# A fused mLSTM, cross-attention and SwiGLU block: the gate columns ride behind the first value strip, the first strip and the late input tiles come in another order, and every large tile starts at a multiple of 512 bytes

## The chip, the cores and the metric

The kernel runs on one core of a Trainium2 chip. The metric is the device time of one execution in microseconds, as the median of several runs. The engines are called by their names in the profile: PE (TensorE, the matrix products), PEld (its weight loads), DVE (VectorE), ACT (ScalarE), POOL (GpSimd) and SP (SyncE, which issues all DMAs here).

## What is computed

One transformer block on x (1024 tokens by 1024 features) with a memory of 256 tokens, all in float32:

```python
h = x
h = h + mlstm_mix(rmsnorm(h, norm_mix), a_w_in, a_conv_w, a_gate_b, a_norm, a_w_out)
h = h + cross_attn(rmsnorm(h, norm_x), rmsnorm(mem, norm_mem), x_w_q, x_w_kv, x_w_o)
h = h + swiglu(rmsnorm(h, norm_ffn), f_w_gate, f_w_up, f_w_down)
out = rmsnorm(h, norm_final)

def mlstm_mix(xn, w_in, conv_w, gate_b, norm_g, w_out):      # 4 heads, key width 128, value width 256
    qk, v, o, g = split(xn @ w_in, [1024, 2048, 3072])       # g: 8 columns, an i and an f gate per head
    qk = silu(causal_dwconv(qk, conv_w))                     # 4 taps
    g = g + gate_b
    i_pre, log_f = g[:4], log_sigmoid(g[4:])
    # a scan over the tokens in chunks, with stabilised exponential gates made of i_pre and cumsum(log_f)
    return (head_rmsnorm(scan(q, k, v, i_pre, log_f), norm_g) * sigmoid(o)) @ w_out
```

## The kernel before

**Products in three terms.** Every large matrix product is made of three float32r products: each operand a is split into a high part ah (a copy written as float32r) and a low part al = a - ah, and a*b is taken as ah*bh + al*bh + ah*bl. ACT writes the high parts, DVE or POOL the low ones. `XH` and `XL` hold the normalised input, transposed (8 blocks `k` of 128 features by 1024 tokens), `WH` and `WL` two weight strips each, used in turn.

**Strips.** The projections are done in strips of 256 weight columns, in the order of the list `STRIPS`: it begins with qk 0, v 0, o 0, then qk 1, v 1, o 1, wo 0, and so on. For each strip SP loads 1 MB into `raw`, ACT copies it into `WH` (`split_hi`, L878), and DVE makes `WL` in two halves (L1606) while PE works on the strip before. A strip has groups `r`, each of which fills one of the PSUM banks 0 to 3 (`NB` = 4) with 24 matmuls of 512 columns, or, for v, with 48 of 256 columns: there the tokens are stationary and the weights are moving. v and o are taken out of PSUM by ACT, qk by DVE, with the convolution (`evac`, L1541 to L1554).

**Order.** It is written out by hand: each engine runs the same loop over `STRIPS` and groups, and at fixed places does the side work that `PARTS` names (`run_parts`): the gates, the scan of the head before, the norms. The scan of head 0 begins with group 0 of the strip qk 1, on PE, ACT and DVE.

**The start.** SP issues four tiles of x (128 tokens each, `xin`), the small vectors, strip 0, the gate weights `wg_raw` (8 columns) and their bias, and then tiles 4 to 7 into the same four buffers, each after PE has turned and ACT has squared the tile that was in it. PE transposes a tile (`turn_x`, L2146), DVE (L1571) and ACT (L1074) take it out of PSUM into `xT`. ACT sums the squares (L883), POOL makes 1/rms (L804), PE spreads it over the partitions (`spread`, L2083), and then `pieces(c, k)` makes one block: DVE multiplies xT, gain and 1/rms (L1463), ACT writes `XH` (L972), and `XL` is made by DVE for even `k` (L1445) and by POOL for odd `k` (L811); c = 0 is the first half of the tokens, c = 1 the second. PE consumes the blocks as they come, in `two_groups` (L1961 to L1963), which does strip qk 0, first half, then second half, with the transposes of the tiles 6 and 7 between.

**The gates.** A product of its own, in `gates` step 0, at the first group of v 0: `wgp` holds the 8 high gate columns, the 8 low ones and zeros, as a stationary operand of 128 columns, against `XH` and `XL` as moving operands (L1974, L1975, 32 matmuls). DVE copies the 16 result rows (L1288), PE transposes them (L1980). Steps 1 to 5 are a chain of short operations that goes back and forth between PE, DVE and ACT; they stand at v 0 groups 2 and 3 and o 0 groups 0, 1 and 3:

```python
for step, (kind, r) in enumerate([("v", 0), ("v", 2), ("v", 3), ("o", 0), ("o", 1), ("o", 3)]):
    part(kind, 0, r, ("gates", step, None))
```

**Places.** All tiles are laid out by hand in one array of SBUF. It starts at byte 1152 of a partition, so that `xT`, `XH`, `XL`, `raw`, `WH`, `WL`, `QK`, `SG`, `YH`, `YL` and `VV` start 128 bytes past a multiple of 512; the part for late tiles (`late_at`, with `W2A`, `VMH` and `KMH`) starts 384 bytes past one.

## Time and profile before

| | |
|---|---|
| median of 3 runs | 1408.13 us (1406.9 to 1408.98) |
| the profiled execution's own time | 1408.76 us |
| its span, first to last instruction | 1407.0 us |
| PE busy | 1373.6 us, 98% of the span |
| PEld / DVE / ACT / POOL busy | 83% / 68% / 35% / 15% |
| TensorE clock granted, mean | 0.992 of full speed |
| DMA | 156.44 MB, mean 111 GB/s |

A busy PE here means that a matmul was in its pipe; since matmuls overlap, how fast it works is read from how many start in a stretch. The profiled execution spent 1.76 us outside the span.

### The profile page before, as it was taken

The numbers are of one execution on the slowest core, as the hardware profiler recorded it, in microseconds if no ns is written. First come the engines' busy times: TensorE is split into PE (matmuls) and PEld (weight loads), VectorE is DVE, ScalarE is ACT, GpSimd is POOL, SyncE is SP. The second block draws the span as 40 slices with busy tenths as digits, with TensorE's granted clock in tenths as the row PEclk, the third lists the DMA queues.
The fourth block names the chain that finished last, engine by engine and source line by source line (L and its number), as shares of the span: only waits on it lengthen the run. The fifth ranks groups of instructions, "written<-read, shape, count | busy, mean of one in ns | idle before, by whom it ended". The sixth has DMA issues, their size and how long they took to land.

```text
span 1407.0 us, 18269 instructions
## 1 busy us (share of the span) xinstructions
PE 1373.6 (98%) x6897; PEld 1165.9 (83%) x6897; DVE 954.8 (68%) x1678; ACT 493.4 (35%) x870; POOL 209.2 (15%) x228
## 2 busy tenths in 40 slices
PE   7999999999999999999999999999999998999997
PEld 6988888889888888888877888888888886888887
DVE  5838458458477884554677976677787778877765
ACT  6323213213335453222344533343444433222222
POOL 4101201201313000000004000000000004444441
PEclk9999999999999999999999999999999999999999
DMA  5110111201313211010132132244444449799702
GB/s 181 34 57 31 56 36 31 60 30 31 106 61 101 80 60 61 31 61 23 38 120 105 47 114 96 74 165 164 142 140 160 153 165 374 246 311 318 236 31 120
DMA packets 109256, 156.44 MB, mean 111 GB/s; under 512 B 6449, under 2 KB 67953, under 8 KB 109169
## 3 DMA queue, kind: packets, MB, share of 16 engines
q1 hardware_dynamic: 109168, 155.28, 32.9%
q8 instruction: 55, 0.90, 0.3%
q14 instruction: 33, 0.26, 0.1%
HBM read 112.79 MB, written 42.47 MB: 110 GB/s over the span
## 4 chain that ended last, share of the span: by engine, by line
PE 88%; DVE 6%; issue 2%; DMA 1%; SPq 1%; ACT 1%; POOL 0%; POOLq 0%; DVEq 0%; ACTq 0%
PE PS L1898 14%; PE PS L1899 14%; PE PS L1900 14%; PE PS L2220 8%; PE PS L2218 8%; PE PS L2219 8%; PE PS L2248 4%; PE PS L2250 4%; PE PS L2249 4%; PE PS L2040 1%; PE PS L2044 1%; PE PS L2042 1%; DVE SG L1430 1%; PE PS L1961 1%; DVE xT L1528 1%
## 5 line engine op out<-in xcount | busy, mean ns | idle before, releaser
L1898 PE MATMUL PS<-XH,WH 128*128 128x512 f32 (+1 forms) x448 | 175.4, 391 | 3.3 <-issue 3.3
L1899 PE MATMUL PS<-XL,WH 128*128 128x512 f32 (+1 forms) x448 | 169.7, 379 | 0.0
L1900 PE MATMUL PS<-XH,WL 128*128 128x512 f32 (+1 forms) x448 | 169.4, 378 | 0.0
L1528 DVE TENSOR_TENSOR xT<-PS,xT 128x512 f32<-128x512 f32 x128 | 87.5, 688 | 47.0 <-PE PS L1900 46.6
L1740 DVE TENSOR_TENSOR xT<-PS,xT 128x512 f32<-128x512 f32 x120 | 80.9, 688 | 43.8 <-PE PS L2250 43.0
L1898 PE MATMUL PS<-YH,WH 128*128 128x512 f32 x256 | 101.5, 396 | 0.7 <-issue 0.7
L1898 PEld LDWEIGHTS PS<-XH,WH 128*128 128x128 f32 x448 | 85.5, 191 | 19.3 <-issue 4.4
L1900 PE MATMUL PS<-YH,WL 128*128 128x512 f32 x256 | 99.8, 390 | 0.0
L1899 PE MATMUL PS<-YL,WH 128*128 128x512 f32 x256 | 99.7, 390 | 0.0
L1900 PEld LDWEIGHTS PS<-XH,WL 128*128 128x128 f32 x448 | 85.4, 191 | 16.0
L1899 PEld LDWEIGHTS PS<-XL,WH 128*128 128x128 f32 x448 | 85.5, 191 | 14.6
L1898 PE MATMUL PS<-WH,XH 128*128 128x256 f32 x320 | 92.6, 289 | 2.0 <-issue 2.0
L1900 PE MATMUL PS<-WH,XL 128*128 128x256 f32 x320 | 90.5, 283 | 0.0
L1899 PE MATMUL PS<-WL,XH 128*128 128x256 f32 x320 | 90.5, 283 | 0.0
L845 POOL TENSOR_TENSOR W2A<-raw,W2A 128x512 fp32r<-128x512 f32 x20 | 27.5, 1377 | 386.6 <-ACT W2A L1185 386.6
L1680 DVE TENSOR_TENSOR U<-PS,U 128x512 f32<-128x512 f32 x50 | 33.6, 688 | 55.7 <-PE PS L2220 55.7
L1606 DVE TENSOR_TENSOR WL<-raw,WH 128x1024 fp32r<-128x1024 f32 x54 | 65.8, 1226 | 3.8 <-ACT WH L878 3.8
L1898 PEld LDWEIGHTS PS<-WH,XH 128*128 128x128 f32 x320 | 61.2, 191 | 2.9 <-issue 2.4
L2220 PE MATMUL PS<-XH,WA 128*128 128x512 f32 x160 | 62.2, 389 | 0.0
L2218 PE MATMUL PS<-XH,WA 128*128 128x512 f32 x160 | 62.2, 389 | 0.0
L2218 PE MATMUL PS<-XH,WB 128*128 128x512 f32 x160 | 62.2, 389 | 0.0
L2220 PE MATMUL PS<-XH,WB 128*128 128x512 f32 x160 | 62.2, 389 | 0.0
(396 smaller groups left out, 3522.7 us busy)
## 6 DMA issues: line engine op xcount, KB each, us to landing
forms_hi<-HS SPq DMA_DIRECT2D x56, 256.0 KB, 2.4
raw<-in_f_w_up_dram SPq DMA_DIRECT2D x11, 1024.0 KB, 5.8
rawE<-in_f_w_gate_dram SPq DMA_DIRECT2D x10, 1024.0 KB, 6.0
raw<-in_f_w_down_dram SPq DMA_DIRECT2D x40, 256.0 KB, 3.8
raw<-in_a_w_in_dram SPq DMA_DIRECT2D x8, 1024.0 KB, 5.3
forms_lo<-U SPq DMA_DIRECT2D x32, 256.0 KB, 2.5
XH<-forms_hi SPq DMA_DIRECT2D x16, 512.0 KB, 6.5
XL<-forms_lo SPq DMA_DIRECT2D x12, 512.0 KB, 7.0
```

Of the source, the lines that this page charges most:

```text
L1528: v.tensor_tensor(xt, PS[:, g % NB, :], xt, ALU.add).then_inc(s_fd, 1)
L1606: last = v.tensor_tensor(WL[:, (n + 1) % 2, at], raw_of(n + 1)[:, at], WH[:, (n + 1) % 2, at].bitcast(F32), ALU.subtract)
L1740: v.tensor_tensor(x, bank_of(g, which), x, ALU.add).then_inc(s_ee, 1)
L1898: mm(dst, wh, xh, start=(k == 0), stop=False)
L1899: mm(dst, wh, xl, start=False, stop=False)
L1900: last = mm(dst, wl, xh, start=False, stop=(k == len(tiles) - 1))
L2218: mm(bank, w[:, i, 0, at], xh[:, kk, :], start=start, stop=False, skip_group_check=True)
L2219: mm(bank, w[:, i, 0, at], xl[:, kk, :], start=False, stop=False, skip_group_check=True)
L2220: last = mm(bank, w[:, i, 1, at], xh[:, kk, :], start=False, stop=stop, skip_group_check=True)
L2248: mm(bank, w[:, i, 0, at], xh[:, u, :], start=start, stop=False, skip_group_check=True)
L2249: mm(bank, w[:, i, 0, at], xl[:, u, :], start=False, stop=False, skip_group_check=True)
L2250: last = mm(bank, w[:, i, 1, at], xh[:, u, :], start=False, stop=stop, skip_group_check=True)
```

## The change

- **Gates in the first value strip.** The strip v 0 is now the first one and qk 0 the second. Its high weights lie in a tile of their own, `GW`, in rows of 272 columns: 256 value columns, 8 high gate columns, 8 low ones. For each block k and tile of 128 tokens, `first_value` does three matmuls: XH by 272 columns, XL by 264, XH by the 256 columns of `WL`. Each of the 8 token tiles has a bank of its own (the eighth takes the fourth's after that is taken out), and comes out of PSUM in two copies, 256 columns to `VV` and 16 to `zg`. The product `wgp`, its copy `grow` and its transposes are gone; the gate chain has 5 steps, at qk 0 group 2 and at o 0 groups 0 to 3.
- **Another start.** Tiles 4 to 7 of x get their own places (`xlate`, where `YH` and `YL` are later), and are issued as soon as tiles 0 to 3 have landed; strip v 0 is loaded in two halves, the second behind tile 5. ACT splits it in two halves, POOL makes the low part of the first half and DVE that of the second. Tiles 4 to 7 are taken out of PSUM by ACT alone, in two halves each, through three banks in turn, and are turned one by one between the blocks k = 0 to 3 of `first_value(0)`. All sixteen `XL` blocks are made by DVE.
- **Places.** `LINE` is 512 in place of 128, and the array's large tiles start at byte 1536, so that `xT` to `VV`, `acc`, `ident` and `late_at` all start at a multiple of 512; the small ones lie ahead of them. `ones`, `tri` and `cmax` lie behind `zg`, behind the gate columns; a column of ones (`one`) takes the place of `ones[:, 0:1]` in `sumsq`.

```diff
-LINE = 128
+LINE = 512
-    STRIPS = [("qk", 0), ("v", 0), ("o", 0)]
+    STRIPS = [("v", 0), ("qk", 0), ("o", 0)]
+    GATED = AT["v", 0]
+    ngroups = lambda n: TT if n == GATED else NGROUPS[STRIPS[n][0]]
+    bank_at = lambda n, r: (0, 1, 2, 3, 4, 5, 6, 3)[r] if n == GATED else GI[n, r] % NB
-    for step, (kind, r) in enumerate([("v", 0), ("v", 2), ("v", 3), ("o", 0), ("o", 1), ("o", 3)]):
-        part(kind, 0, r, ("gates", step, None))
+    part("qk", 0, 2, ("gates", 0, None))
+    for step in range(1, 5):
+        part("o", 0, step - 1, ("gates", step, None))
-        who = "dve" if c in (2, 3) or (c < 2 and k % 2 == 0) or (c == 5 and k >= KT // 2) else "pool"
+        who = "dve" if c in (2, 3) or c < 2 or (c == 5 and k >= KT // 2) else "pool"
+        small_at = (nc.sbuf_base + 31) // 32 * 32
+        base = (small_at + 4 * SMALL + LINE - 1) // LINE * LINE
...
+        GW = sb_at("GW", [P, KT, SW + 2 * GCOLS], late_at, F32R)
+        zg = sb_at("zg", [P, TT, 2 * GCOLS], late_at + 8704)
+        ones = sb_at("ones", [P, P], late_at + 11264)
...
SP:
-            for t in range(TT):
-                if t >= 4:
-                    sp.wait_ge(s_turn, t - 3)
-                    sp.wait_ge(s_sq, t - 3)
-                sp.dma_start(xin[t % 4], x_t[t]).then_inc(s_xin[t % 4], 16)
...
+            sp.dma_start(dst[:, 0:KT // 2], src[:, 0:KT // 2]).then_inc(s_w0, 16)
+            sp.dma_start(wg_raw, cols(a_w_in, G0, 2 * H)).then_inc(s_wg, 16)
+            for t in range(4):
+                sp.wait_ge(s_xin[t], 16)
+                sp.dma_start(xlate[t], x_t[4 + t]).then_inc(s_xin[t], 16)
+                if t == 1:
+                    sp.dma_start(dst[:, KT // 2:], src[:, KT // 2:]).then_inc(s_wdma, 16)
+            sp.dma_start(gbias[:, :], a_gate_b[0:1, :].to_broadcast([P, 2 * H])).then_inc(s_gb, 16)
+            sp.wait_ge(s_wl0, 1)
ACT:
+            split_first(0)
             for k in range(KT):
                 pieces(0, (k,))
+                if k == 0:
+                    split_first(1)
+                if 1 <= k <= 4:
+                    late_tile(k + 3)
+                if 2 <= k <= 5:
+                    square_x(k + 2)
+            for k in range(KT):
+                pieces(1, (k,))
+                if 1 <= k <= 4:
+                    evac(GATED, FIRST_OUT[k - 1])
+                if 4 <= k <= 5:
+                    split_second(k - 4)
DVE:
+            pieces(0, (0,))
+            pieces(0, (1,))
+            dve.wait_ge(s_wg, 16)
+            link(v.tensor_copy(GW[:, :, SW:SW + GCOLS], wg_raw))
+            v.tensor_tensor(GW[:, :, SW + GCOLS:], wg_raw, GW[:, :, SW:SW + GCOLS].bitcast(F32), ALU.subtract).then_inc(s_wgs, 1)
+            pieces(0, (2, 3))
+            dve.wait_ge(s_whi, 1)
+            v.tensor_tensor(by_k(WL[:, 0, second]), by_k(raw[:, second]), GW[:, KT // 2:, 0:SW].bitcast(F32),
+                            ALU.subtract).then_inc(s_wlo, 1)
+            pieces(0, range(4, KT))
             pieces(1, range(KT))
PE:
+            def first_value(half, between=None):
+                wide, narrow = SW + 2 * GCOLS, SW + GCOLS
+                for kk in range(KT):
+                    if between is not None:
+                        between(kk)
+                    lo_ready(pe, half, kk)
+                    for r in range(half * NT, half * NT + NT):
...
+                        mm(bank[:, 0:wide], xh, GW[:, kk, 0:wide], start=(kk == 0), stop=False, skip_group_check=True)
+                        mm(bank[:, 0:narrow], xl, GW[:, kk, 0:narrow], start=False, stop=False, skip_group_check=True)
+                        last = mm(bank[:, 0:SW], xh, col(GATED, kk, 0, SW)[1], start=False, stop=(kk == KT - 1),
+                                  skip_group_check=True)
-                if step == 0:
-                    pe.wait_ge(s_wgs, 1)
-                    for half in range(NHALF):
-                        for kk in range(KT):
...
-                            mm(PS[:, NB + half, :], wgp[:, kk, :], xh, start=(kk == 0), stop=False)
-                            last = mm(PS[:, NB + half, :], wgp[:, kk, :], xl, start=False, stop=(kk == KT - 1))
             def late_tiles(kk):
+                if 1 <= kk <= 3:
+                    turn_x(4 + kk)
                 if kk == 4:
                     wait_strip(0)
                 if kk == 7:
                     spread(0, 1)
+            turn_x(4)
             pe.wait_ge(s_wl0, 1)
+            pe.wait_ge(s_wgs, 1)
+            first_value(0, late_tiles)
+            first_value(1)
```

## Rows read from the trace of the kernel before

**Rows 1.** The page, busy time of PE.

```profile
PE 1373.6 (98%) x6897; PEld 1165.9 (83%) x6897; DVE 954.8 (68%) x1678; ACT 493.4 (35%) x870; POOL 209.2 (15%) x228
```

**Rows 2.** Table by stretch: PE, PEld, DVE, ACT, POOL busy (starts), clock, DMA share, GB/s.

```profile
17.80:44.50 26.70, 25.77 (x119) 20.83 (x118) 20.31 (x33) 15.77 (x25) 14.01 (x12) 0.96 0.15 45
44.50:51.80 7.30, 7.30 (x34) 6.02 (x33) 7.12 (x10) 0.96 (x2) 0.00 (x0) 1.00 0.03 6
...
76.10:98.90 22.80, 22.80 (x101) 18.27 (x100) 9.75 (x38) 5.73 (x9) 0.00 (x0) 1.00 0.15 47
98.90:1407.00 1308.10, 1283.91 (x6393) 1087.85 (x6391) 895.45 (x1558) 454.05 (x811) 187.95 (x198) 0.99 0.33 112
52.00:62.00 10.00, 10.00 (x86) 10.00 (x85) 9.47 (x19) 3.55 (x4) 0.00 (x0) 1.00 0.31 102
```

**Rows 3.** The same table, two stretches at half the clock.

```profile
16.55:19.97 3.42, 3.42 (x13) 3.03 (x13) 3.38 (x5) 2.76 (x7) 3.14 (x3) 0.50 0.47 192
753.80:760.70 6.90, 6.90 (x20) 5.55 (x20) 0.16 (x1) 0.00 (x0) 1.20 (x2) 0.51 0.40 139
```

**Rows 4.** The timeline of the start: start us, length us, engine, line, operation.

```profile
5.67 3.23 SPq L592 DMA_DIRECT2D QK<-in_a_w_in_dram  x1
...
10.94 1.78 SPq L585 DMA_DIRECT2D VQ<-in_x_dram  x4
...
12.71 1.91 ACT L878 ACTIVATE WH<-raw 128x2048 fp32r<-128x2048 f32 x1 [2.64 <-DMA raw<-in_a_w_in_dram]
...
14.70 2.96 POOL L766 TENSOR_TENSOR WL<-raw,WH 128x512 fp32r<-128x512 f32 x2 [3.23 <-ACT WH L878]
...
15.13 1.09 PE L2146 MATMUL PS<-ident,VQ 128*128 128x128 f32 x8 [2.96 <-DMA VQ<-in_x_dram]
15.18 1.35 DVE L1445 TENSOR_TENSOR XL<-SG,XH 128x512 fp32r<-128x512 f32 x1 [1.29 <-ACT XH L972]
15.57 1.04 ACT L883 ACTIVATE QK<-VQ 128x1024 f32<-128x1024 f32 x1
...
16.61 0.57 ACT L1074 ACTIVATE xT<-PS 128x512 f32<-128x512 f32 x1
...
17.90 0.77 PE L1961 MATMUL PS<-XH,WH 128*128 128x512 f32 x1
```

**Rows 5.** The timeline, one block of the second half.

```profile
32.09 1.29 ACT L972 ACTIVATE XH<-SG 128x512 fp32r<-128x512 f32 x2 [3.03 <-DVE SG L1463]
...
32.75 0.69 DVE L1445 TENSOR_TENSOR XL<-SG,XH 128x512 fp32r<-128x512 f32 x1
33.36 1.40 DVE L1463 SCALAR_TENSOR_TENSOR acc<-xT,vcols,PS 128x512 f32<-128x512 f32 x2
```

**Rows 6.** The timeline of DVE, convolutions of group 0 and group 3.

```profile
41.06 0.75 DVE L1541 TENSOR_SCALAR acc<-PS,vcols 128x512 f32<-128x512 f32 x1
...
44.20 0.16 DVE L1554 COPY small<-PS 128x3 f32<-128x3 f32 x1
...
55.11 0.75 DVE L1541 TENSOR_SCALAR acc<-PS,vcols 128x512 f32<-128x512 f32 x1
...
59.02 0.16 DVE L1554 COPY small<-PS 128x3 f32<-128x3 f32 x1
```

**Rows 7.** The timeline of DVE, gate steps 1 and 4.

```profile
64.08 0.23 DVE L1295 COPY ks<-PS 128x64 f32<-128x64 f32 x1 [1.37 <-PE PS L1980]
...
67.14 1.22 DVE L1606 TENSOR_TENSOR WL<-raw,WH 128x1024 fp32r<-128x1024 f32 x1
...
82.12 0.19 DVE L1324 COPY hs<-PS 128x32 f32<-128x32 f32 x1 [3.04 <-PE PS L1992]
...
86.28 0.27 DVE L1336 TENSOR_SCALAR hs<-SG,hs 32x128 f32<-32x128 f32 x1
```

**Rows 8.** The groups by line and shape: busy us, mean ns of one.

```profile
L2040 PE MATMUL PS<-VV,wT 128*128 128x257 f32 x64 | 19.2, 382 | 0.0
L2042 PE MATMUL PS<-Cst,qs 128*128 128x257 f32 x56 | 16.7, 380 | 0.0
```

More of the change, by code:

```diff
@@ L54, in build_block @@
     FIRST, FREED, took = {}, [], {"act": 0, "dve": 0, "up": 0}
-    GROUPS = [(n, r) for n, (kind, _) in enumerate(STRIPS) for r in range(NGROUPS[kind])]
+    GATED = AT["v", 0]
+    assert GATED == 0
+    ngroups = lambda n: TT if n == GATED else NGROUPS[STRIPS[n][0]]
+    GROUPS = [(n, r) for n in range(len(STRIPS)) for r in range(ngroups(n))]
     at = GROUPS.index((NF, 0))
@@ L219, in build_block @@
         half_neg = few(NT)
+        one = few(1)
         nsum, nmean, nrms = few(NHALF, NT), few(NHALF, NT), few(NHALF, NT)
@@ L282, in build_block @@
         sqsum = [None, halves(QK[:, 1, 1, :]), SG[:, :, HALF:]]
-        wgp = YH[:, 0, :].rearrange("p (k g) -> p k g", k=KT)
-        grow = VV[0:4 * H, 1].rearrange("p t d -> p (t d)")[:, 0:S]
+        XT4 = sb_at("XT4", [P, 4, S], place["YH"])
+        xlate = [XT4[:, t, :] for t in range(4)]
         fout = xin
@@ L827, in _ @@
                 kind, h = STRIPS[n]
-                for r in range(NGROUPS[kind]):
+                for r in range(ngroups(n)):
                     run_parts(n, r, todo)
@@ L885, in gates @@
             def gates(step, b):
-                if step == 1:
+                if step == 0:
                     act.wait_ge(s_gd, 1)
@@ L1076, in _, with split_first @@
-            square_x(0)
-            square_x(1)
-            square_x(2)
-            square_x(3)
-            split_hi(0)
+                for unit in range(2):
+                    dst, src = tile_of(t, unit)
+                    sc.activation(dst, src, ACT.Copy).then_inc(s_xta, 1)
+            def split_first(u):
+                k = slice(u * KT // 2, (u + 1) * KT // 2)
+                src = raw[:, u * KT * P:(u + 1) * KT * P].rearrange("p (k n) -> p k n", k=KT // 2)
+                if u == 0:
+                    act.wait_ge(s_w0, 16)
+                    sc.activation(GW[:, k, 0:SW], src, ACT.Copy).then_inc(s_w0h, 1)
+                else:
+                    act.wait_ge(s_wdma, 16)
+                    sc.activation(GW[:, k, 0:SW], src, ACT.Copy).then_inc(s_whi, 1)
@@ new lines, in split_second @@
+            def split_second(u):
+                if u == 0:
+                    act.wait_ge(s_wdma, 16 * DMAS[1][1])
+                at = slice(u * KT * P, (u + 1) * KT * P)
+                last = sc.activation(WH[:, 1, at], raw[:, at], ACT.Copy)
+                if u:
+                    last.then_inc(s_whi, 1)
+            for k in range(KT):
[4 more added lines that the diff above has]
+                    split_second(k - 4)
@@ L1090, in _ @@
                 kind, h = STRIPS[n]
-                for r in range(NGROUPS[kind]):
+                for r in range(ngroups(n)):
                     if r == 0 and held and STRIPS[held[0][0]][0] == "q":
@@ L1595, in _ @@
                 which = 1 if kind == "wo" else 2
-                for r in range(NGROUPS[kind]):
+                for r in range(ngroups(n)):
                     run_parts(n, r, todo)
@@ L1609, in _ @@
                             last.then_inc(s_wlo, 1)
+                        elif n == GATED:
+                            last.then_inc(s_wl0, 1)
                     if kind == "mv":
@@ L1889, in wait_bank, with product @@
                 if g >= NB:
-                    who, count = FREED[g - NB]
+                    who, count = FREED[NT - 1 if TT <= g < TT + NT - 1 else g - NB]
                     pe.wait_ge({"act": s_fa, "dve": s_fd, "up": s_hf}[who], count)
-            def product(dst, tiles, before=None):
+            def product(dst, tiles, before=None, second=None):
                 for k, ((wh, wl), (xh, xl)) in enumerate(tiles):
+                    if second is not None and k == len(tiles) // 2:
+                        wait_strip(second)
                     if before is not None:
@@ L1945, in group @@
                     order = range(KT) if before is None else EARLY + LATE
-                    last = product(bank, [(col(n, kk, r % 2), xpart(kk, at, HALF)) for kk in order], before)
+                    last = product(bank, [(col(n, kk, r % 2), xpart(kk, at, HALF)) for kk in order], before,
+                                   second=1 if (n, r) == (1, 0) else None)
                 last.then_inc(s_mm, 1)
@@ L2067, in sumsq @@
                 for t in range(NT):
-                    last = mm(X2[:, t:t + 1], sqsum[which][:, half, t * P:(t + 1) * P], ones[:, 0:1], start=True, stop=True)
+                    last = mm(X2[:, t:t + 1], sqsum[which][:, half, t * P:(t + 1) * P], one, start=True, stop=True)
                 last.then_inc(s_ssq, 1)
@@ L2176, in _ @@
                     run_parts(n, r, todo)
-                    if r == 0:
+                    if r == 0 and n == 1:
+                        pe.wait_ge(s_whi, 2)
+                        pe.wait_ge(s_wl0, 2)
+                    elif r == 0:
                         wait_strip(n)
```

218 lines of the change are left out of this document (101 added, 117 removed).

## The prediction

> **What bounds the kernel now.** I read the page first: PE is busy for 98% of the span [rows 1]. A busy PE need not be fast, so the second view is the table by stretch, for how many matmuls start. From 44.5 to 51.8 us the 32 matmuls of 512 columns of the gate product fill the stretch with next to nothing left, 0.227 us from start to start; from 52 to 62 us some 84 of 256 columns fill it, 0.12 us each [rows 2]. Hence a column costs (0.227 - 0.12) / 256 = 0.42 ns, and each matmul about 0.013 us on top. From 44.5 to 51.8 and from 76.1 to 98.9 us PE has no idle time at all, and over the remaining 1308.1 us it is idle for 24 [rows 2]. So until 98.9 us, where strip qk 1 and with it the scan of head 0 begin, a column that PE need not stream is time won, unless another engine is late with what PE wants next. Third, the timeline of the start: PE waits for tile 4 of x until 15.13 us and begins its first product at 17.90 us, when POOL has the first half of WL (14.70 + 2.96) [rows 4]. From there to 44.5 us it is idle for 0.93 of 26.7 us [rows 2].
>
> The code behind the start of qk 1 is the same before and after but for places, so I work out when qk 1 starts: 98.9 us before.
>
> **The gates' columns.** Removed: 32 matmuls of 512 columns, the stretch 44.5 to 51.8 us, 7.3 us [rows 2], and 8 transposes of 16 columns: between nothing and 8 x 0.12 = 1 us, the start-to-start time of the 256-column matmuls; they are far narrower, so I take 0.5. Added: in each of 64 steps (8 blocks, 8 token tiles) 16 + 8 = 24 more columns, 64 x 24 x 0.42 ns = 0.65 us. By this alone the change gains about 7.1 us. DVE's copy of `grow` goes, ACT gets eight small copies; neither is on PE's path there.
>
> **The start.** SP issues x0 to x3, the vectors and now only half of the strip, so the gate columns, whose issue alone takes 3.23 us [rows 4], go out some 0.5 us earlier, at 5.1 us, and tile 4 behind them at about 8.4 instead of 10.94 us. Before, tile 4 landed at 15.13 us, 4.2 us after its issue into empty queues [rows 4]; that would make it 12.6 now, but it also waits behind half a strip and the gate columns: I take 13.2 us. Each further 0.5 MB I estimate at 1.25 us: tile 5 at 14.4, the second half of the strip at 15.7, tiles 6 and 7 at 17 and 18. The first half strip lands at about 10.8 us (the whole one was there at 12.71). ACT splits it in half of 1.91 us, to 11.8 us, and POOL needs 2.96 us for its two subtractions [rows 4]: 14.8 us. DVE's four tile copies are as before; I estimate their end at 12.3 us. Then come two blocks' products at 0.7 us [rows 5], one XL block, and the gate columns. That XL block took 1.35 us at 15.18 us while POOL worked, and takes 0.69 us at 32.75 us without it [rows 4, 5]. I take the long value, since POOL's second subtraction overlaps it again: `s_wgs` at 15.7 us. **First product at 15.7 us, before 17.9.**
>
> The Trainium skill (SBUF — State Buffer, Who interferes with whom) says that a DVE instruction with two SBUF inputs and a GpSimd instruction that reads SBUF block each other for the whole instruction. The row of 1.35 us agrees. By that rule moving all sixteen XL blocks to DVE also rids them of POOL, which has no work left after 15 us.
>
> **First half of the tokens.** PE needs per block 4 x (0.12 x 3 + 24 x 0.42 ns) = 1.48 us, eight times 11.8 us, and 3 late tiles of 1.0 us and the spread of 0.6 us: 15.5 us. But ACT now takes out both halves of each late tile. From the landing of the second half strip at 15.7 us it has, in its own order: that split, 0.95 us; seven XH blocks at 0.6 us; eight half tiles at 0.57 us; four squares at 1.04 us [rows 4, 5]: 13.9 us, so XH of block 7 is there at 29.6 us. Followed in order, block 4 is ready on ACT at 24.5, block 5 at 27.3, block 6 at 28.95 us; each needs 0.7 us more on DVE. PE has done block 3 at 24.8 us, waits 0.4 us for block 4, 1.3 us for block 5 and 0.1 for block 6, ends block 6 at 31.1 us, spreads, and ends block 7 at 33.2 us. DVE is no bound here: 1.4 us a block.
>
> **Second half.** Block 0 comes after the spread: 0.7 us DVE, 0.64 us ACT, 0.7 us DVE [rows 5], so PE starts it at 33.9 us (before there was a like wait). Then DVE makes a block in 1.4 us [rows 5] where PE needs 1.48, and DVE's share of 0.7 us more per odd block, taken over from POOL, is hidden; ACT has the blocks, four outputs and the next split, 10 us in all. 33.9 + 11.9 = 45.8 us: **strip qk 0 starts at 45.8 us**. WL of qk 0, DVE's last work before, is ready by halves at about 45 and 46 us, and PE wants the second half only after four blocks.
>
> **Strips qk 0 and o 0.** Let T be the start of qk 0. Four groups of 24 matmuls with 0.1 us for the change of group: 22.1 us. DVE is the one that is late now. The groups end at T + 5.7, 11.2, 16.6 and 22.1 us. A convolution took 3.3 us in groups 0 and 1 (41.06 to 44.36) and 4.1 us in 2 and 3 (55.11 to 59.18) [rows 6]. At group 2 DVE first does the old gate step 1, 3.1 us with its trip to ACT (64.08 to 67.14), and half of a WL, 1.15 us [rows 7]; so convolution 2 ends at T + 23.5, `finish_qk` of group 1 at 24.1, convolution 3 at 28.2, `finish_qk` of group 2 at 28.8 us, and only then comes gate step 1 of the new count: T + 29.3 us. PE would want that result for the second group of o 0 at T + 22.1 + 0.4 + 5.55 = T + 28.0 us. **A new wait of 1.3 us.** Behind it the steps fit: the step with the long chain takes 4.4 us (82.12 to 86.55) [rows 7], and a group of o is 5.5 us, so 0.7 us is left after PE's own small product. o 0 takes 22.8 us as before [rows 2], plus the 0.4 us of the first step, plus 1.3, plus 0.2 for the steps closer together: T + 46.8 = 92.6 us. SP's loads of strips 1 to 3 have over 15 us each.
>
> **Sum.** 98.9 - 92.6 = 6.3 us. By parts: the gates 7.1; the first product starts 2.2 earlier; the wait in o 0 costs 1.3; the waits of the first halves are about 1.7 us longer than before. The profiled execution took 1408.76 us with a span of 1407.0, 0.6 us above the median shown; the difference goes on the median: 1408.13 - 6.3 = 1401.8 us.
>
> **Alignment.** By layout, all big tiles start 128 bytes past a multiple of 512 before. `VV` is the moving operand at sixteen offsets 1028 bytes apart, `Cst` at a single one: 382 and 380 ns [rows 8]. So the start of an operand moves a matmul by 0 to 2 ns. I take 0. GW's rows are 1088 bytes apart, so its operands are not at multiples of 512; at 2 ns each 128 of them cost 0.3 us. No row shows a large operand at a multiple of 512, so a gain is not excluded; its upper bound is the whole fixed part of 0.013 us.
>
> **The rivals.**
> 1. *The gain is lost at the start* (21%): every us by which the second half strip lands later than 15.7 us goes through ACT's 13.9 us chain to T. It stands behind the gate columns, tile 4 and tile 5 in the queues. From a landing at 19.2 us on the gain is below 2.8 us; I take 20 us, hence 1408.1 - 2.0 = 1406.1 us. For it: tile 4 took 4.2 us with empty queues. Against: the second half strip is 3.5 MB into a transfer of which 3 MB, the four tiles and the whole strip, were there at 12.71 us before [rows 4].
> 2. *Half clock through the first half* (6%), the case on the other side. PE ran at clock 0.50, its lower level of 1.2 GHz, from 16.55 to 19.97 us after its wait for tile 4, and at 0.51 for 6.9 us from 753.8, with 20 starts instead of 30 [rows 3]. The new first half has more small waits (PE 15.5 of 17.5 us) than the old start (25.8 of 26.7). If it stays at half clock from 15.7 us on, its blocks take 24 instead of 12 us and its transposes 6 instead of 3.5: it ends at 46 instead of 33.2 us, and the whole at 1401.8 + 12.8 = 1414.6 us. Half clock costs half of its length, less the 1.8 us of waits that it fills; to get past 1410.9 us it must last 22 us. Against: the two stretches are 3.4 and 6.9 us long.
> 3. *The places make every product faster* (4%): if the fixed 0.013 us came from operands that cross a multiple of 512 and fell away, some 6,200 of the 6,897 matmuls [rows 1] (an estimate: all but transposes and the scan) gain it: 81 us, 1321 us. Against: rows 8, where offsets make no difference.
> 4. *The new places are dear* (4%), and the change does not do what its name says: if the residue 0 cost 2 ns, the upper bound above, on each of some 6,200 products, that is 12.4 us, 1414.2 us. It decides from 1.5 ns on. Against: rows 8 show the 2 ns between many offsets and one, not between residues.
>
> The Trainium skill (TensorE: Matmul & The Clock Gate, Back-to-back issue gap) gives N / 2.4 GHz plus 2.5 ns for a warm matmul. That is 0.216 us for 512 columns where the trace has 0.227; were alignment what is missing, the rule would leave 2.5 ns of the 13 and make rival 3 worth 65 us instead of 81. The trace disagrees with it for this kernel at the offsets it has.
>
> **How the numbers follow.** Forecast 65%, rivals 21, 6, 4, 4. The forecast's own range is 1399.5 to 1404.5: the wait in o 0 may be 0 or 3 us, ACT's chain 1.5 us shorter or longer, and stretches at half clock elsewhere shift by 1.7 us (half of 3.4) either way [rows 3]. The range reaches into rival 1: 1399.0 to 1407.5. What this kernel's measurement can tell from no change is about 0.2%, 2.8 us. Faster: forecast and rival 3, less a little for the forecast's own tail, 68%; same: rival 1 and that tail, 22%; slower: rivals 2 and 4, 10%.
>
> **What would show it.** Right: no L1974 line; PE's first product near 15.7 us; qk 0 near 45.8; short waits of PE for XL around 25 to 28 us; one wait of 1 to 2 us for DVE ahead of the second group of o 0; qk 1 near 92.6; matmuls of 512 columns still 0.227 us apart. Wrong: the second half strip landing after 19 us; a longer stretch at half clock; a spacing other than 0.227; or waits after qk 1 that were not there.

## The result, and the profile after

The kernel after takes **1398.34 us**, median of 4 runs (1396.8 to 1400.0), where the kernel before takes 1408.4 us (4 runs, 1406.9 to 1408.98). The ratio is 0.993, 95% interval 0.9913 to 0.9948. I had forecast 1401.8 us with a range from 1399.0 to 1407.5: the sign of the gain is as forecast and it arises ahead of strip qk 1, but its size is 10.1 us instead of 6.3, and the median lies 0.66 us below the range.

The page of the kernel after, busy time of PE and number of matmuls, against [rows 1]:

```profile
PE 1360.5 (98%) x6857; PEld 1154.8 (83%) x6857; DVE 955.6 (69%) x1682; ACT 495.8 (36%) x888; POOL 194.9 (14%) x218
```

The table by stretch of the kernel after (columns as in [rows 2]): the first half of the tokens, the second half, strip qk 0, strip o 0, and all from strip qk 1 on.

```profile
14.90:32.00 17.10, 15.55 (x125) 14.97 (x125) 11.96 (x18) 13.84 (x27) 1.22 (x2) 1.00 0.32 94
32.00:43.75 11.75, 11.75 (x97) 11.75 (x97) 10.63 (x17) 7.53 (x21) 0.00 (x0) 1.00 0.01 2
43.75:65.55 21.80, 21.80 (x98) 18.02 (x97) 12.77 (x25) 6.87 (x11) 0.00 (x0) 1.00 0.22 63
65.55:90.30 24.75, 23.58 (x106) 18.63 (x105) 16.97 (x56) 5.22 (x9) 0.00 (x0) 1.00 0.24 73
90.30:1395.00 1304.70, 1280.70 (x6393) 1085.26 (x6391) 895.79 (x1558) 454.32 (x811) 187.88 (x198) 1.00 0.33 113
```

The same 6393 matmuls stand behind the start of strip qk 1, which is now at 90.30 us and was at 98.90 [rows 2]: **8.6 us are gained ahead of it.** Behind it the two profiles differ by 3.4 us (1308.1 against 1304.7). Most of that is one place: the stretch of 6.9 us at half clock from 753.8 us [rows 3] has no counterpart. In the kernel after the same work runs at clock 1.00, with 38 starts in 7.2 us where [rows 3] has 20 in 6.9:

```profile
744.80:752.00 7.20, 7.20 (x38) 6.11 (x39) 0.69 (x2) 0.51 (x2) 1.21 (x2) 1.00 0.42 141
```

The timeline of the start of the kernel after, against [rows 4]:

```profile
4.58 0.43 SPq L601 DMA_DIRECT2D raw<-in_a_w_in_dram  x1
5.05 0.50 SPq L602 DMA_DIRECT2D QK<-in_a_w_in_dram  x1
5.60 2.39 SPq L605 DMA_DIRECT2D XT<-in_x_dram  x2
8.03 0.44 SPq L607 DMA_DIRECT2D raw<-in_a_w_in_dram  x1
...
11.41 2.51 POOL L783 TENSOR_TENSOR WL<-raw,GW 128x512 fp32r<-128x512 f32 x2
...
13.62 0.85 DVE L1483 TENSOR_TENSOR XL<-SG,XH 128x512 fp32r<-128x512 f32 x1
14.48 1.06 ACT L1100 ACTIVATE GW<-raw 128x1024 fp32r<-128x1024 f32 x1 [0.89 <-DMA raw<-in_a_w_in_dram]
14.93 0.36 PE L2024 MATMUL PS<-GW,XH 128*128 128x272 f32 x1 [1.85 <-DVE GW L1614]
16.46 1.03 PE L2201 MATMUL PS<-ident,XT 128*128 128x128 f32 x8
17.54 1.09 ACT L1089 ACTIVATE xT<-PS 128x512 f32<-128x512 f32 x2
```

The gate columns (L602) cost SP 0.50 us, not 3.23; tile 4 goes out at 5.60 us (with tile 5 in one line here, 2.39 us for both), the second half strip at 8.03. Tile 4 is there by 11.98 us, when PE transposes it (forecast 13.2). The second half strip is there at 14.48 us (forecast 15.7), the first product starts at 14.93 us (forecast 15.7). The last two lines, the transposes of tile 5 and ACT's copy of them, matter below.

The table of waits of the kernel after, 12 to 92 us, with total, times and longest: PE's two waits for XL, one at block 5 of the first half (25.28 to 26.02 us) and one ahead of the second half (31.19 to 31.97 us), and the new wait in strip o 0.

```profile
PE PS L2024 <- DVE XL L1483: 1.5, 2, 0.8
PE PS L2038 <- DVE acol L1348: 1.2, 1, 1.2
```

This view counts a wait from the end of the matmul before. Below, waits are counted from the time at which the next matmul would have started at the usual spacing, which gives 0.1 to 0.2 us more: 0.9, 0.9 and 1.33 us.

### The profile page after: what moved, and what is told of

The parts are those of the page before. It is cut to its first block, busy times and chain, and to the rows that moved or that the text cites. A ratio compares the mean times of both kernels' runs of the same rounds, so it can differ in the third digit from the quotient of the medians.

```text
span 1395.0 us, 18199 instructions
## 1 busy us (share of the span) xinstructions
PE 1360.5 (98%) x6857; PEld 1154.8 (83%) x6857; DVE 955.6 (69%) x1682; ACT 495.8 (36%) x888; POOL 194.9 (14%) x218
## 4 chain that ended last, share of the span: by engine, by line
PE 86%; DVE 7%; issue 2%; DMA 2%; ACT 1%; SPq 1%; POOL 0%; POOLq 0%; DVEq 0%; ACTq 0%
PE PS L1938 14%; PE PS L1940 14%; PE PS L1939 14%; PE PS L2277 8%; PE PS L2279 8%; PE PS L2278 8%; PE PS L2307 4%; PE PS L2309 4%; PE PS L2308 4%; PE PS L2089 1%; PE PS L2093 1%; PE PS L2091 1%; DVE SG L1468 1%; DVE xT L1565 1%; DMA xT<-forms 1%
## 5 line engine op out<-in xcount | busy, mean ns | idle before, releaser
L1938 PE MATMUL PS<-XH,WH 128*128 128x512 f32 (+1 forms) x480 | 186.6, 389 | 3.4 <-issue 3.3
L1940 PE MATMUL PS<-XH,WL 128*128 128x512 f32 (+1 forms) x480 | 181.0, 377 | 0.0
L1939 PE MATMUL PS<-XL,WH 128*128 128x512 f32 (+1 forms) x480 | 180.9, 377 | 0.0
L1565 DVE TENSOR_TENSOR xT<-PS,xT 128x512 f32<-128x512 f32 x128 | 87.6, 689 | 47.0 <-PE PS L1940 46.5
L1938 PEld LDWEIGHTS PS<-XH,WH 128*128 128x128 f32 x480 | 90.8, 189 | 20.1 <-issue 4.4
L1940 PEld LDWEIGHTS PS<-XH,WL 128*128 128x128 f32 x480 | 90.7, 189 | 17.0
L1939 PEld LDWEIGHTS PS<-XL,WH 128*128 128x128 f32 x480 | 90.8, 189 | 15.7
L1938 PE MATMUL PS<-WH,XH 128*128 128x256 f32 x256 | 74.3, 290 | 2.0 <-issue 2.0
L1940 PE MATMUL PS<-WH,XL 128*128 128x256 f32 x256 | 72.4, 283 | 0.0
L1939 PE MATMUL PS<-WL,XH 128*128 128x256 f32 x256 | 72.4, 283 | 0.0
L1718 DVE TENSOR_TENSOR U<-PS,U 128x512 f32<-128x512 f32 x50 | 33.6, 688 | 55.7 <-PE PS L2279 55.7
L1718 DVE TENSOR_TENSOR SG<-PS,SG 128x512 f32<-128x512 f32 x50 | 33.5, 686 | 34.3 <-PE PS L2279 34.3
```

The lines of the kernel that those rows point to most:

```text
L1565: v.tensor_tensor(xt, PS[:, g % NB, :], xt, ALU.add).then_inc(s_fd, 1)
L1718: v.tensor_tensor(q[dst], bank_of(s, which), q[other], ALU.add).then_inc(s_dd, 1)
L1938: mm(dst, wh, xh, start=(k == 0), stop=False)
L1939: mm(dst, wh, xl, start=False, stop=False)
L1940: last = mm(dst, wl, xh, start=False, stop=(k == len(tiles) - 1))
```

## The experiments

Twelve runs in three series, each series on a chip of its own with the kernel before beside it: 1405.45 us (11 runs), 1406.81 us (21) and 1407.88 us (17). Single executions of one kernel spread over 2 to 7 us, as stretches at half clock fall into them or not, so effects of 2 us are read from the trace, as the times at which PE reaches a given matmul ("qk 0 at 43.94 us" is the time at which PE starts that strip).

The times can also be freed of the clock. A straight line through the times of a series against the mean granted clock of each execution, with one slope for all kernels, has a slope of 0.88, 0.88 and 0.96 us per 0.001 of the clock, and its distances between kernels are called differences **at equal clock** below (with 95% intervals). They are estimates, since the clock is recorded to 0.001.

**1. The change again.** No edit.

> The changed kernel as it is, for the granted clock of each run beside the kernel before on the same chip. Theory A (the front alone): the true gain is the 8.6 us by which strip qk 1 starts earlier (98.92 against 90.29 us in the two traces), and what the medians show beyond it, 1.5 us, is stretches at half clock that fall differently from run to run; then the median lies 8 to 10.5 us under the kernel before, and the time of a run follows its mean clock, about 2.8 us for 0.002 of the clock. Theory B (the places speed up products or keep the clock up everywhere): the time from 90.3 us to the end is shorter than before in every run, 11 to 13 us gain with the clock always at 0.997.

Measured: 1398.57 us, ratio 0.9945 (0.9932 to 0.9958); qk 0 at 43.94, qk 1 at 90.51 us. The third series asked once more:

> The kernel after, unchanged, on a third chip or day: the first two series gave 0.9930 (0.9913 to 0.9948) and 0.9945 (0.9932 to 0.9958) of the kernel before. Theory (7.8 to 8.6 us are gained ahead of strip qk 1 in every execution, and the rest of any difference is how many stretches at half clock fall into the executions compared): first product 14.9 to 15.8 us, qk 0 at 43.8 to 44.6 us, qk 1 at 90.3 to 91.2 us, ratio 0.9930 to 0.9948. Rival (my forecast of 6.3 us is the true gain, and the first series was lucky): qk 1 later than 92 us or a ratio above 0.9950.

Measured: 1397.12 us, ratio 0.993 (0.9912 to 0.9949); first product 14.86, qk 0 at 43.68, qk 1 at 90.21 us. At equal clock the kernel after is 7.2 us faster than the kernel before in the first series and 7.3 in the third (each within 0.9 us), where the medians differ by 6.9 and 10.8. Its profile has one stretch at half clock behind qk 1 before the end (from 1176.4 us), and the 6393 matmuls take 1303.10 us:

```profile
90.20:1393.30 1303.10, 1279.41 (x6393) 1084.02 (x6391) 895.84 (x1558) 454.26 (x811) 187.54 (x198) 1.00 0.33 113
```

**2. The kernel before again.**

> The kernel before, unchanged, for a second trace and the clocks of several executions. In the first profile strip qk 1 starts at 98.92 us, with PE at half clock from 16.55 to 19.97 us on the way there, and again in stretches at 508, 753.8 (6.9 us long) and 1190.7 us. Theory A (the change gains some 8.6 us ahead of qk 1 in every execution, the rest is clock): qk 1 starts at 98.9 us again within 0.4 us, and what the time differs from the first profile's is the length of the half clock stretches behind it. Theory B (part of the 8.6 us is the half clock stretch of the start, which falls in some executions only): where the stretch at 16 us is missing, qk 1 starts 1.0 to 1.7 us earlier, at 97.2 to 97.9 us, and the gain of the change ahead of qk 1 is then about 7 us, which is what the second series of times showed (1405.45 against 1398.57 us).

Measured: 1406.73 us; qk 1 at 99.59 us, with half clock from 13.7 to 20.5 us. Together with experiment 10 below three profiles of before have qk 1 at 98.92, 99.59 and 98.82 us, three of after at 90.29, 90.51 and 90.21: 8.3 to 9.4 us apart, 8.8 in the mean. All three profiles of before have a stretch at half clock between 13 and 21 us, and so has experiment 5's, the fourth in the old order: there it is the rule. In the new order two of ten profiles have one. So the stretch of theory B is real, but it belongs to the old start (see the last section). In the first profile PE's products run at half clock from 17.90 to 19.97 us; I estimate its price at half of these 2.07 us, about 1 us, which leaves some 7.6 of the 8.6 us.

**3. Places.** The large tiles at 128 and (with 32 in the first added line) at 32 bytes past a multiple of 512, the new order kept:

```diff
-        base = (small_at + 4 * SMALL + LINE - 1) // LINE * LINE
+        base = (small_at + 4 * SMALL + LINE - 1) // LINE * LINE + 128
-            top[0] = (top[0] + LINE - 1) // LINE * LINE
+            top[0] = base + (top[0] - base + LINE - 1) // LINE * LINE
```

> The changed kernel with all its large tiles 128 bytes past a multiple of 512, where they were before; nothing else differs. If the places matter to nothing: the same time as the changed kernel within 0.1%, matmuls of 512 columns 0.227 us apart in both. If the multiple of 512 is what brought a part of the gain, or keeps the clock up around 750 us: 2 to 4 us slower than the changed kernel.

> The changed kernel with all its large tiles 32 bytes past a multiple of 512, a residue that neither kernel has. If the places matter to nothing: the same time within 0.1%. If operands off a multiple of 128 or 512 cost: by the upper bound of 2 ns on 6,200 products up to 12 us slower, with a start-to-start time of 0.229 us.

Measured: 1399.72 us, ratio 0.9956 (0.9942 to 0.9969), and 1397.32 us, 0.9939 (0.9926 to 0.9952), around the 0.9945 of the kernel after. Strip qk 0 for residue 128, for 32, and for 0 (the kernel after): as many matmul starts in as long a time.

```profile
44.50:60.00 15.50, 15.50 (x70) 12.81 (x70) 8.52 (x15) 3.79 (x7) 0.00 (x0) 1.00 0.22 69
```
```profile
44.70:60.20 15.50, 15.50 (x70) 12.81 (x69) 8.54 (x15) 3.76 (x7) 0.00 (x0) 1.00 0.23 69
```
```profile
43.80:59.30 15.50, 15.50 (x70) 12.81 (x70) 8.51 (x15) 3.79 (x7) 0.00 (x0) 1.00 0.23 69
```

So the places do nothing for PE. They do something for the loads. The second half strip landed at 14.61 us in the same series with the tiles at multiples of 512 (14.46 to 14.61 in seven profiles, experiment 6's aside), and here at 15.26 us (residue 128) and 15.42 us (residue 32), as the timeline of ACT shows for each:

```profile
15.26 1.06 ACT L1100 ACTIVATE GW<-raw 128x1024 fp32r<-128x1024 f32 x1 [1.28 <-DMA raw<-in_a_w_in_dram]
```
```profile
15.42 1.06 ACT L1100 ACTIVATE GW<-raw 128x1024 fp32r<-128x1024 f32 x1 [1.34 <-DMA raw<-in_a_w_in_dram]
```

SP issued that half at 8.17 and 8.27 us here and at 8.50 us in experiment 1. The strip's 1024 packets of 1 KB took 50.0 and 50.2 ns each in the mean, in the eight other profiles in the new order 46.0 to 47.7. Strip qk 0 starts at 44.44 and 44.62 us, 0.5 and 0.7 us later than in experiment 1. At equal clock the two kernels are 1.0 us (within 0.8) and 0.4 us (within 0.9) slower than the kernel after. One profile of each residue is little, but later loads point the same way: from 100 to 1300 us the packets of 2 KB took 90.2 to 91.2 ns in the mean in the six profiles with the tiles off a multiple of 512 (these two and the four in the old order), and 88.5 to 89.4 in the eight others. Why they take longer is not shown.

**4. Gate step 0 earlier**, so that DVE's step 1 is not what PE waits for:

```diff
-    part("qk", 0, 2, ("gates", 0, None))
+    part("qk", 0, 0, ("gates", 0, None))
```

> The changed kernel with gate step 0 at group 0 of qk 0 instead of group 2, where DVE has 5.7 us free. If the wait of 1.33 us ahead of the second group of o 0 comes from DVE being late by these 3.1 us, it goes and qk 1 starts at about 89.0 instead of 90.3 us, 1.3 us faster. Rival: ACT or DVE is late elsewhere by then (ACT's split of strip o 0 waits for the gate step), the wait moves and the time stays.

Measured: 1397.32 us (1393.73 to 1400.38), ratio 0.9938. The wait of 1.33 us is gone: qk 1 comes 45.2 us after qk 0 instead of 46.5, and at equal clock this kernel is 0.9 us (within 0.8) faster than the kernel after. But in this profile qk 0 itself is late, at 45.40 us, because PE fell to half clock right after its first products. The table by stretch and the timeline of this run:

```profile
15.30:18.70 3.40, 3.40 (x18) 3.40 (x17) 2.66 (x5) 2.31 (x5) 0.00 (x0) 0.51 0.27 101
```
```profile
17.46 1.67 PE L2201 MATMUL PS<-ident,XT 128*128 128x128 f32 x8
19.17 1.09 ACT L1089 ACTIVATE xT<-PS 128x512 f32<-128x512 f32 x2 [1.57 <-PE PS L2201]
```

18 starts in 3.4 us where the kernel after has 31 in the same stretch. The transposes of tile 5 end at 19.1 us instead of 17.5, and ACT, which copied that tile at 17.54 us, copies it at 19.17 us. All later work up to qk 0 is 1.6 us late.

**5. Most of the gate product left out, in the old order.**

```diff
-                        for kk in range(KT):
+                        for kk in range(1):
...
```

> The kernel before with 28 of the 32 gate matmuls of 512 columns left out (only the first of the eight blocks of the features is summed into the gates; the rest of the gate product is left out). Theory A (PE's columns are worth their full time on this path): 28 x 0.227 = 6.36 us less, qk 1 starts at 92.6 us and the time falls by 6.4 us. Rival: DVE's convolutions, which are late by then, are what the gate product covers. The step that now runs behind v 0 would then show a PE wait and the gain is below 5.5 us.

Measured: 1404.62 us, ratio 0.9995 (0.9982 to 1.0009), and qk 1 at 99.93 us, no earlier than in experiment 2; at equal clock 1.7 us (within 0.6) faster than the kernel before, not 6.4. My theory falls here and its rival holds. The timeline of DVE and PE, and the table by stretch, of this run:

```profile
43.73 1.21 DVE L1606 TENSOR_TENSOR WL<-raw,WH 128x1024 fp32r<-128x1024 f32 x1
44.86 0.74 DVE L1541 TENSOR_SCALAR acc<-PS,vcols 128x512 f32<-128x512 f32 x1
45.64 2.31 DVE L1544 SCALAR_TENSOR_TENSOR acc<-PS,vcols,acc 128x511 f32<-128x511 f32 x3
...
48.66 1.22 DVE L1606 TENSOR_TENSOR WL<-raw,WH 128x1024 fp32r<-128x1024 f32 x1
...
49.98 0.55 PE L1898 MATMUL PS<-WH,XH 128*128 128x256 f32 x1 [4.92 <-issue]
```
```profile
44.90:49.98 5.08, 0.16 (x1) 0.03 (x1) 4.94 (x9) 0.63 (x1) 0.00 (x0) 0.94 0.00 0
49.98:56.20 6.22, 6.22 (x29) 6.22 (x30) 5.80 (x12) 0.63 (x1) 0.00 (x0) 0.50 0.57 173
```

PE starts nothing for 5.08 us and is idle for 4.92 of them: strip v 0 cannot start before DVE has the second half of its WL (48.66 + 1.22), and between the halves of that WL DVE has the convolution of group 1. In the old order the gate product was PE's work for all of the time that DVE needed, and little more. Of 28 x 0.227 = 6.36 us only 6.36 - 5.08 = 1.3 are left, and the 6.8 us at half clock from 49.4 us, which begin in the standstill, took those back and more (qk 1 at 99.93 us, in the first profile of before 98.92).

**6. The second half strip later.** It is issued behind tiles 6 and 7 (`if t == 3:` for `if t == 1:` ahead of its `dma_start`).

> The kernel after, with the second half of the first strip issued behind tiles 6 and 7 of x and not ahead of them. It should land 2 to 2.7 us later than 14.48 us. My chain (ACT's own order from the landing of that half to the last block of the first half, then to qk 0): qk 0 starts later by as much as the half strip lands later, since ACT stands waiting for it ahead of the second block: 43.75 + 2 to 2.7 us, time 1398.5 + 2 to 2.7 us. Rival: PE's own work sets the first half, and ACT's order has slack (PE waits only 2 us there): then qk 0 moves by less than 1 us.

Measured: it is there at 16.89 us, 2.41 later, and qk 0 starts at 46.06 us, 2.31 later: theory confirmed. (1398.8 us, ratio 0.9941 with 0.9928 to 0.9955: the medians do not resolve these 2.3 us; at equal clock this kernel is 5.4 us, within 1.0, faster than the kernel before, where the kernel after has 7.2 and 7.3.) The timeline of ACT:

```profile
16.89 1.06 ACT L1100 ACTIVATE GW<-raw 128x1024 fp32r<-128x1024 f32 x1 [2.82 <-DMA raw<-in_a_w_in_dram]
```

**7. The odd XL blocks back on POOL** (`LO` and POOL's `pieces` calls as before the change).

> The kernel after, with the odd XL blocks of the product of the tokens back on POOL, as before the change. Theory A (POOL and DVE hold each other up): DVE's long forms come back (1.35 us instead of 0.7 for the XL block while POOL subtracts, the scaled products above 0.7 us), PE waits longer in the first half, qk 0 starts 0.5 to 3 us later than 43.75 us, time up by as much. Rival (the shift to DVE only loads DVE with 8 x 0.7 us more, and POOL would have done them beside it): qk 0 starts at the same time or up to 1 us earlier.

Measured: 1398.21 us, ratio 0.9933 (0.9915 to 0.995), qk 0 at 45.74 us. Of these 2.0 us 1.5 are a stretch at half clock from 15.6 us, as in experiment 4: tile 5 is copied at 19.02 us. From there to qk 0 it is 26.7 us where all other kernels have 26.2. The timeline of this run shows where the 0.5 us arises, at block 5:

```profile
26.80 1.27 POOL L827 TENSOR_TENSOR XL<-SG,XH 128x512 fp32r<-128x512 f32 x1 [3.77 <-ACT XH L986]
...
28.12 0.39 PE L2028 MATMUL PS<-GW,XH 128*128 128x272 f32 x1 [1.37 <-POOL XL L827]
```

POOL takes 1.27 us for a block that takes DVE 0.69, and PE waits for it: it is POOL's own slowness and not contention that shows, since DVE is idle then. So theory A's late start came, but at this block not by its mechanism. Where the two engines do overlap DVE becomes longer (last section), but there it has time to spare.

**8. Tile 4 copied out by DVE**, right behind the gate columns, and no more by ACT; gate step 0 early as in experiment 4:

```diff
-                if 1 <= k <= 4:
+                if 2 <= k <= 4:
                     late_tile(k + 3)
...
+            dve.wait_ge(s_turn, 5)
+            for unit in range(2):
+                dst, src = tile_of(4, unit)
+                v.tensor_copy(dst, src).then_inc(s_xt, 1)
             pieces(0, (2, 3))
```

> The kernel after with two repairs: the first gate step one group of strip qk 0 after another is left where it is but gate step 0 goes from group 2 to group 0 of qk 0 (this alone removed PE's wait of 1.33 us for acol), and both halves of the transposed tile 4 of x are copied out by DVE, ahead of its third block, and not by ACT. If ACT's chain sets the start of qk 0, taking 1.1 us off it moves qk 0 about 1.0 us earlier, to 42.7 us, and with the wait in o 0 gone qk 1 starts at 88.0 us; time 1396.2 us where the kernel after has 1398.5, ratio to before about 0.9925. Rival (DVE, which then has 1.2 us more ahead of block 2, becomes the late one): PE waits at block 2 or 4 and qk 0 starts no earlier than 43.6 us.

Measured: 1397.66 us, ratio 0.9928 (0.991 to 0.9947), 0.9930 for the kernel after beside it. The wait in o 0 is gone (45.2 us from qk 0 to qk 1 at 89.32 us), but qk 0 starts at 44.09 us, not at 42.7: ACT, relieved of 1.1 us, waits 1.0 us for DVE's third block and then for PE's transposes of tile 5, and copies them at 17.89 us. PE began 0.3 us later here (15.26 us). No gain from this part. The medians of this version and the kernel after do not differ by more than their spread; at equal clock it is 1.4 us (within 1.0) faster, about the 1.33 us of the wait.

**9. 32 matmuls more, in the new order.**

```diff
             first_value(1)
+            for j in range(32):
+                mm(PS[:, 7, :], GW[:, j % KT, 0:P], XH[:, j % KT, HALF:S], start=True, stop=True, skip_group_check=True)
```

> The kernel after with 32 matmuls of 512 columns added between strip v 0 and strip qk 0, whose sums nobody reads (extra work, nothing left out). Theory (in the new order nothing is hidden behind PE ahead of qk 0, so the columns cost their full time): strip qk 0 starts 7.2 to 7.3 us later, qk 1 too, time up by 7.3 us, almost back at the kernel before. Rival (the columns cover other engines' work here as they did in the old order, where leaving out 6.36 us of them gave 1.3 us): up by less than 3 us.

Measured: 1405.65 us, 8.5 us above the kernel after beside it, ratio to before 0.9993 (0.9979 to 1.0006); at equal clock 7.9 us (within 0.9) above. In its profile tile 5 is copied at 17.89 us, qk 0 starts at 51.52 us: 33.6 us later where it is 26.2 without them, 7.4 us for 32 x 0.227 = 7.3 us. The table by stretch shows them fill the time, DVE idle (34 starts, its third pair of numbers 0.00):

```profile
44.10:51.50 7.40, 7.40 (x34) 6.01 (x33) 0.00 (x0) 2.57 (x5) 0.00 (x0) 1.00 0.48 142
```

Here a column is worth its full time, where experiment 5 found a fifth of it. This run is also close to the new start and order alone, without the removal: as many columns as before ahead of qk 1, which comes at 98.1 us, 0.8 us earlier than before. The removal alone (experiment 5) gains 1.3 us, both together 8.6.

**10. Gate columns issued ahead of the strip, in the old order** (the two issues change places).

> The kernel before with the gate columns issued ahead of the first strip and not behind it. Theory (SP's 3.23 us on that load were the queues being full behind four tiles and a whole strip, not the load's own cost): its issue takes 0.5 to 1 us now, and the wait moves to the strip's issue, which takes some 3 us; tile 4's issue stays at 10.5 to 11 us, its landing near 15 us. Rival (narrow rows of 32 bytes cost SP 3.2 us wherever they stand): 3 us again for the gate columns, and the strip lands later by that.

Measured in one execution: the timeline of SP's queue.

```profile
4.66 0.43 SPq L591 DMA_DIRECT2D QK<-in_a_w_in_dram  x1
5.13 3.63 SPq L579 DMA_DIRECT2D raw<-in_a_w_in_dram  x2
```

Of the strip's two halves the second takes 3.01 of these 3.63 us. So the 3 us are paid by whatever SP issues at 5.7 us: behind 3 MB in the kernel before, behind 2.5 MB and the gate columns here. Whether bytes or the number of packets make SP wait, these runs do not separate. Tile 4 is issued 1.4 us earlier than in [rows 4], at 9.54 us, and is transposed at 14.91 us, 0.2 earlier; qk 1 at 98.82 us.

## Why the prediction was wrong

**The sum.** One term of it was mis-sized: the start of strip qk 0, 45.8 us forecast, 43.75 measured. Two steps made it late by about 1.2 and 1.1 us: the landing of the second half strip, and ACT's chain behind it. And one effect that I had put at nothing takes part in the first: the places. The rest up to qk 1 holds to 0.3 us (T + 46.8 against T + 46.54). So qk 1 came 8.6 us earlier instead of 6.3. That alone would have given 1399.5 us, inside the range by 0.5; the remaining 1.5 us of the difference between the medians arise behind qk 1, where the two profiles differ by one stretch at half clock, and are not a step of the change.

**Landing of the second half strip: 15.7 forecast, 14.48 measured.** One error is in the sentence that the gate columns' "issue alone takes 3.23 us". I read the duration of an issue as its own cost. It was SP waiting behind what it had issued (experiment 10: 0.43 us in another place, 0.50 in the kernel after). With it went tile 4 at 8.4 us: SP issued it at 5.60, and it was there by 11.98 instead of 13.2. The other is "I take 0" for the places: I looked at matmul operands alone and not at what the loads write. With the tiles where they were before, 128 bytes past a multiple of 512, the half strip lands at 15.26 us (experiment 3), so that some 0.65 to 0.8 of the 1.2 us go with the places.

**ACT's chain: 13.9 us forecast, 12.8 measured.** From the landing to the end of XH of block 7 (26.66 + 0.6 us). I added durations. ACT starts the next instruction before the one ahead has ended: one tile with its block and its square takes 2.51 us from start to start (19.55 to 22.07 in the kernel after) where the durations I used give 0.6 + 2 x 0.57 + 1.04 = 2.78. PE's waits for blocks 4 to 6 were 0.1, 0.9 and 0.1 us (forecast 0.4, 1.3, 0.1), and 0.9 us ahead of the second half (forecast 0.7).

**What sets qk 0** was half seen. In nine of the ten profiles in the new order qk 0 starts 26.2 us after ACT copies tile 5 (7.4 more with experiment 9's matmuls); the tenth, experiment 7's, has 26.7. That copy starts at the later of two times: when ACT is through with the split of the second half strip, a block, tile 4 and a block (experiment 6), 3.0 us after that split begins, or when PE has transposed tile 5, 2.6 us after its first product (experiment 8, and experiment 4 with half clock in between). The forecast had the first alone. In the kernel after both fall together, at 17.5 us, which is why taking work off ACT alone gained nothing.

**The gates' columns.** In the new order they are worth what I said: 32 such matmuls cost 7.4 us (experiment 9), less the 0.65 for the wider products. "By this alone the change gains about 7.1 us" was wrong as an account of the parts: in the old order their removal is worth 1.3 us (experiment 5). With v 0 going first, ACT empties its PSUM banks, and DVE's convolutions stand no longer between it and the next WL: in the kernel after DVE has the last half of that WL at 42.88 us (41.66 + 1.22, the line below), 0.9 us before PE wants it. The removal and the new order gain together what neither gains alone (1.3 us in experiment 5, 0.8 in experiment 9, 8.6 together).

```profile
41.66 1.22 DVE L1642 TENSOR_TENSOR WL<-raw,WH 128x1024 fp32r<-128x1024 f32 x1
```

The condition I wrote down myself, "unless another engine is late", was not asked of the old order. PE has no idle time there, but DVE has the second half of WL of v 0 at 50.4 us only, 1.4 us before PE wants it at 51.8, as the timeline of DVE in the kernel before shows:

```profile
45.41 0.74 DVE L1541 TENSOR_SCALAR acc<-PS,vcols 128x512 f32<-128x512 f32 x1
...
49.21 1.22 DVE L1606 TENSOR_TENSOR WL<-raw,WH 128x1024 fp32r<-128x1024 f32 x1
```

**The wait in o 0**: 1.3 us forecast, 1.33 measured, at the place and for the instruction named. Experiments 4 and 8 remove it.

**The rivals.** 1, the gain lost at the start: the rule behind it holds (experiment 6, 2.41 us give 2.31), the landing went the other way. 2, half clock through the first half: it comes in two of ten profiles, for 3.4 us, and costs some 1.6; nowhere longer. It was argued from the many small waits of the new start; what the profiles show is that the one longer wait ahead of the first product counts, and the change made that shorter. 3 and 4, the places and the matmuls: experiment 3, nothing either way; what the places do to the loads was no rival of mine.

**How much is gained.** Ahead of qk 1 the gain is 8.3 to 9.4 us in the profiles; the medians differ by 10.1 us in the first measurement, 6.9 in the first series and 10.8 in the third. The clock explains this spread: the executions of the kernel before had a mean granted clock of 0.9949 in the first series and 0.9934 in the third, those of the kernel after 0.9952 and 0.9958, and at equal clock both series give the same, 7.2 and 7.3 us. That is less than the 8.8 us of the profiles, since the half clock of the old start lowers the clock of the kernel before and is taken out with it. It is part of the 98.9 us from which I forecast, and so no error of mine. Of the 3.8 us by which the first measurement passes my 6.3, 2.3 are the two steps above and 1.5 stretches at half clock behind qk 1, which is luck. By the ratio of the first series the time would be 1400.4 us, inside my range, with the same two steps wrong.

**What stays open.** Why packets take longer with the tiles off a multiple of 512 no run here shows, nor whether that costs any time behind qk 1, where the stretches at half clock hide effects of this size.

## What to carry to other kernels

A PE without idle time does not prove that its columns are what costs: look for the time at which each other engine would have had PE's next operand ready, and the distance from there to PE's start of it is all that a removal gains. Estimate a chain on one engine from start to start of its instructions in the trace, and take the issue time of a DMA behind megabytes of others for waiting. Where two chains meet at a late copy, shorten both or neither. Compare times of a few microseconds only at the same mean clock. When tiles move, ask of the loads too what the new place does.

## What the runs showed of the hardware

- **No effect of an operand's place on matmuls.** Residues 0, 32 and 128 give 0.227 us per matmul of 512 columns, and the 257-column products over `VV` take 382 ns before [rows 8] and with every residue after. The Trainium skill (TensorE: Matmul & The Clock Gate, Back-to-back issue gap) gives 512 / 2.4 + 2.5 = 216 ns for an isolated warm matmul; the 11 ns more that all kernels here show are not the placement. For the loads into the same tiles see experiment 3: 46.0 to 47.7 ns for a packet of 1 KB at multiples of 512, 50.0 and 50.2 ns off them.
- **Half clock after a standstill.** Over the 14 profiles from 12 us on (their last microseconds aside) PE has 211 waits of at least 0.5 us (counted as in the table of waits) and 36 stretches at half clock, of 3.4 or 6.8 us. Each stretch begins close to the end of one of the longer waits, from 1.6 us before it to 1.4 us behind it. Of 154 waits of 0.5 to 1.65 us none is followed by one, of 38 waits of 1.8 to 2.1 us 18 are, of 19 waits of 2.5 to 4.9 us 18. The stretches near 500, 745 and 1180 us stand behind waits of 2.05, 1.9 and 2.7 us; the one in experiment 5 stands at a wait of 4.92 us. At the start the old order has waits of 2.5 to 3.0 us and half clock in four of four profiles, the new order 1.8 to 2.1 us and half clock in two of ten. One such wait and stretch in the kernel before, the timeline of PE and the table by stretch:

```profile
1190.12 0.47 PE L2248 MATMUL PS<-XH,W2B 128*128 128x512 f32 x1 [2.73 <-DVE xT L1740]
```
```profile
1190.70:1194.10 3.40, 3.40 (x10) 2.63 (x9) 1.36 (x2) 0.70 (x2) 3.40 (x3) 0.51 1.06 383
```

- **DVE beside POOL.** In the kernel after the XL block at 13.62 us begins when POOL's subtraction has 0.30 us left (11.41 + 2.51 = 13.92) and takes 0.85 us; alone it takes 0.69. The Trainium skill (SBUF — State Buffer, Who interferes with whom) says that two such instructions exclude each other for their whole length; by an estimate from that rule the block would take 0.30 + 0.69 = 0.99 us. The traces agree with the rule but for a constant 0.14 us: DVE's instruction is longer by what POOL's had left when DVE's began, less 0.14 us (0.137 to 0.148 in the 30 such overlaps of four profiles in which POOL had at least 0.15 us left). That is 0.16 us more for 0.30 left here, 0.66 for 0.80 at the row of 1.35 us that the prediction names (the first of POOL's two subtractions runs from 14.70 to 15.98 us), and 0.87 for 1.01 in experiment 7, where a half of WL that takes 1.23 us in the kernel after takes 2.09:

```profile
41.16 1.29 POOL L827 TENSOR_TENSOR XL<-acc,XH 128x512 fp32r<-128x512 f32 x1 [0.69 <-ACT XH L986]
```
```profile
41.44 2.09 DVE L1646 TENSOR_TENSOR WL<-raw,WH 128x1024 fp32r<-128x1024 f32 x1
```
